# Mixing stage of a two-block transformer kernel: the first pair of attention scores placed after weight unit 14 instead of 13

## The reference, cut to what matters

```python
proj = u @ w_in                     # 1024 -> 5120 columns
q_a, k_a, v_a, q_b, k_b, v_b, g_a, g_b = jnp.split(proj, cuts, axis=-1)
q_a, k_a = partial_rotary(...), partial_rotary(...)
y_a = moba_attention(q_a, k_a, v_a)             # 8 heads, causal softmax here
y_b = stick_breaking_attention(q_b, k_b, v_b)   # 8 heads
merged = gate_a * (y_a @ w_branch_moba) + gate_b * (y_b @ w_branch_sb)
return merged @ w_out
```

## Time and profile before

| | |
|---|---|
| median of three executions | 1198.6 us |
| the profiled execution, its own time | 1198.96 us |
| its span, first to last instruction | 1197.1 us |
| PE busy | 1190.7 us, 99% |
| DVE busy | 782.6 us, 65% |
| ACT busy | 705.6 us, 59% |
| GpSimd busy | 74.1 us, 6% |
| chain that ended last: PE's share | 95% |
| chain that ended last: a DMA transpose of q and k (`qkT`) | 1% |

### The profile page before, as it was taken

How to read it: one execution, slowest core, us unless ns; L and a number is a source line. 1 busy time by engine, 2 the same in 40 slices (tenths; PEclk the granted TensorE clock), 3 DMA queues, 4 the chain that set the end, 5 groups by cost and what they waited for, 6 DMA issues and landing times.

```text
span 1197.1 us, 16770 instructions
## 1 busy us (share of the span) xinstructions
PE 1190.7 (99%) x5582; PEld 983.5 (82%) x5582; DVE 782.6 (65%) x1113; ACT 705.6 (59%) x1035; POOL 74.1 (6%) x119
## 2 busy tenths in 40 slices
PE   9999999999999999999999999999999999999998
PEld 7888888777788888888888788888888888888887
DVE  6655655798676555656778756755656666765554
ACT  7655555776656554557766567655555556655552
POOL 0430000000000000001220110000000000000000
PEclk9999999999999999999999999999999999999999
DMA  9977765795476888755656528977755453876662
GB/s 323 275 225 235 223 197 157 195 186 183 142 224 186 255 252 235 223 171 168 201 172 181 176 70 236 251 225 218 211 168 176 141 181 104 263 225 200 202 198 76
DMA packets 229176, 237.34 MB, mean 198 GB/s; under 512 B 76864, under 2 KB 169152, under 8 KB 229120
## 3 DMA queue, kind: packets, MB, share of 16 engines
q1 hardware_dynamic: 163792, 214.61, 57.2%
q10 hardware_dynamic: 63536, 16.26, 8.2%
q0 software_dynamic: 1792, 5.75, 1.6%
HBM read 219.78 MB, written 1.05 MB: 184 GB/s over the span
## 4 chain that ended last, share of the span: by engine, by line
PE 95%; ACT 1%; DVE 1%; DMA 1%; issue 1%; ACTq 0%; POOL 0%; SPq 0%; POOLq 0%
PE bank L2149 29%; PE bank L2151 29%; PE bank L2150 29%; PE bank L2208 2%; DMA sb_qkT<-sb_qkT 1%; PE bank L2356 1%; PE bank L2611 1%; DVE sb_wl L1444 1%; PE bank L2628 1%; PE bank L2372 1%; PE bank L2343 1%; ACT sb_wh L761 1%; PE bank L2341 0%; ACTq L1041 0%; PE bank L2310 0%
## 5 line engine op out<-in xcount | busy, mean ns | idle before, releaser
L1444 DVE TENSOR_TENSOR sb_wl<-sb_raw,sb_wh 128x1024 fp32r<-128x1024 f32 x313 | 376.4, 1222 | 122.9 <-ACT sb_wh L761 117.7
L2149 PE MATMUL bank<-sb_wh,sb_aTh 128*128 128x512 f32 (+1 forms) x1124 | 435.8, 388 | 0.5 <-DVE sb_aTl L1866 0.4
L2151 PE MATMUL bank<-sb_wh,sb_aTl 128*128 128x512 f32 (+1 forms) x1124 | 430.9, 383 | 0.0
L2150 PE MATMUL bank<-sb_wl,sb_aTh 128*128 128x512 f32 (+1 forms) x1124 | 430.7, 383 | 0.0
L761 ACT ACTIVATE sb_wh<-sb_raw 128x1024 fp32r<-128x1024 f32 (+1 forms) x319 | 327.1, 1047 | 154.1 <-PE bank L2151 101.2
L2149 PEld LDWEIGHTS bank<-sb_wh,sb_aTh 128*128 128x128 f32 x1124 | 211.2, 188 | 42.6 <-DVE sb_aTl L1866 0.8
L2151 PEld LDWEIGHTS bank<-sb_wh,sb_aTl 128*128 128x128 f32 x1124 | 211.2, 188 | 41.8
L2150 PEld LDWEIGHTS bank<-sb_wl,sb_aTh 128*128 128x128 f32 x1124 | 211.4, 188 | 40.2
L1444 DVE TENSOR_TENSOR sb_wl<-sb_z,sb_wh 128x1024 fp32r<-128x1024 f32 x88 | 107.4, 1225 | 55.9 <-ACT sb_wh L761 55.8
L881 ACT ACTIVATE sb_junk<-bank,sb_rstd 128x256 f32<-128x256 f32 x88 | 37.0, 471 | 156.9 <-PE bank L2151 156.7
L1507 DVE SCALAR_TENSOR_TENSOR sb_scores<-bank,sb_rstd,sb_junk 128x256 f32<-128x256 f32 x88 | 38.5, 479 | 118.1 <-ACT sb_junk L881 118.1
(11 more groups left out here) (231 smaller groups left out, 930.3 us busy)
## 6 DMA issues: line engine op xcount, KB each, us to landing
sb_raw<-ffn_w_down SPq DMA_DIRECT2D x80, 256.0 KB, 4.4
sb_raw<-w_in SPq DMA_DIRECT2D x80, 256.0 KB, 3.7
sb_raw<-w_down SPq DMA_DIRECT2D x80, 256.0 KB, 3.9
sb_raw<-w_gate SPq DMA_DIRECT2D x48, 256.0 KB, 3.2
sb_raw<-w_up SPq DMA_DIRECT2D x48, 256.0 KB, 3.9
sb_raw<-ffn_w_gate SPq DMA_DIRECT2D x44, 256.0 KB, 3.6
sb_raw<-ffn_w_up SPq DMA_DIRECT2D x44, 256.0 KB, 4.4
sb_raw<-e_w_in SPq DMA_DIRECT2D x40, 256.0 KB, 3.3
```

Source lines behind the costliest of these rows:

```text
L1444: dve.tensor_tensor(wl[:, u % NSPLIT, :], raws[SLOT[u]], wh[:, u % NSPLIT, :].bitcast(F32), ALU.subtract).then_inc(low_done, 1)
L2149: pe.matmul(dst, lh, w_hi, start=start, stop=False)
L2150: pe.matmul(dst, lh, w_lo, start=False, stop=False)
L2151: return pe.matmul(dst, ll, w_hi, start=False, stop=stop)
```

## The change

One number of the first list is changed. Pair 0 (heads 0 and 1, both stick-breaking) is scored after unit 14 instead of unit 13.

```diff
-        MIX_SCORES = [13, 17, 21, 25, 29, 32, 35, 38]
+        MIX_SCORES = [14, 17, 21, 25, 29, 32, 35, 38]
         MIX_T = [17, 18, 21, 22, 25, 26, 29, 30, 32, 33, 35, 36, 38, 39, 40, 41]
```

## The result

The changed kernel took 1202.66 us at the median of seven runs (1201.1 to 1203.46) against 1198.6 before: ratio 1.0032, 95% interval [1.0022, 1.0042], 4.1 us slower. Predicted were 1200.3 us and a range of 1199.2 to 1201.9, so the direction was right and the size was not. The profiled execution took 1202.5 us with a span of 1200.7.

The account below looks back on a forecast made before the run. TensorE, busy for 99% of the span, was taken to bound the kernel. A removed wait (-0.70 us) and a new one (+2.40) gave +1.7 on 1198.6, so 1200.3 us, range 1199.2 to 1201.9.

Parts of the forecast that it names:

- -0.70 + 2.40: TensorE's removed wait for joined q and k, less 0.70 us, plus a new 2.40 us wait before head 1's transposes.
- The new wait (steps 1 to 7): Chain from pair 0's scores through VectorE and ScalarE to TensorE's transposes of head 1, which wait 2.40 us.
- steps 3 and 4: On VectorE, evac(3), rotate(3) and unit 19's split come before the sums of head 1, which start at 237.88.
- steps 6 and 7: ScalarE's copy pt_step(0), behind unit 21's split and qk_split(2), ends at 243.91; head 1's transposes wait 2.40 us for it.
- What goes: TensorE's wait at pair 0's scores for VectorE's join of turned q and k disappears, gaining at most 0.70 us.
- Rival (b), the clock: TensorE's clock drops in the longer wait before head 1's transposes: 1.96 us more, +3.7 in all, 1202.3 us; chance 0.07.
- Rival (c), a second wait: Slack of 0.6 us before head 3's transposes at step 22 runs out; for one microsecond past it, +2.7, 1201.3; chance 0.10.
- Rival (a), the gain kept: Copy pt_step(0) ends by 241.5, so no new wait before head 1's transposes; 0.7 us gained, 1197.9 us; chance 0.10.

Follow-up runs that it names:

- Experiment 1: Changed kernel, with VectorE's sums of head 1 put back ahead of evac(3) and the rotation at step 16: 1198.62 us, ratio 0.9998.
- experiment 4: Changed kernel, with ScalarE's copy of head 0's turned probabilities moved to the head of step 17: 1200.40 us, ratio 1.0014.
- experiment 6: The kernel before, unchanged, run again over eleven runs: 1198.62 us, ratio 1.0000.
- experiment 10: The changed kernel, unchanged, one further execution: 1202.89 us.
- experiment 7: The changed kernel, unchanged, run again over eleven runs: 1201.58 us, ratio 1.0025.
- experiments 2 to 4: Changed kernel with TensorE's wait filled, 1201.12 us; kernel before with only TensorE's scores moved, 1199.72 us; changed kernel with ScalarE's copy first, 1200.40 us.
- experiment 2: Changed kernel, with eight unused 512-column matmuls on TensorE ahead of the transposes of head 1: 1201.12 us, ratio 1.0018.
- experiments 6, 8 and 9: The kernel before, unchanged, run again (eleven runs, then one execution each): 1198.62, 1198.45 and 1198.95 us.

## Why the prediction was wrong, point by point

Predicted were +1.7 us as -0.70 + 2.40; measured were 4.06. Two steps failed. The removed wait was counted in full and is about nothing near the median, and the fall of the clock, which cost 1.6, stood outside the sum as a rival with a chance of 0.07. The 2.40 was right, and 2.40 + 1.6 is 4.0.

*The new wait (steps 1 to 7).* Right. VectorE takes the scores 0.95 after TensorE starts them (0.96 predicted), the last exp of head 1 starts 11.80 after the scores (11.82), the copy 15.07 (15.16), and the wait by TensorE's starts is 2.68 - 0.23 = 2.45 us (2.40). Experiment 1 took it away by the order of VectorE (steps 3 and 4) and experiment 4 by that of ScalarE (steps 6 and 7).

*What goes.* The removed wait is 0.70 us in the execution that the rows come from, and no typical one. This term was mis-sized: it is 0.0 to 0.1 in three further traces, and near the median about nothing. I subtracted a wait that the landing of a DMA ends as if it were the same in each execution. The time of the profiled run gave no sign of it: it lay 0.36 above the median, but the traced run of experiment 6 lies 0.37 above its own median and has no such wait. Without the term the sum is +2.4 to +2.5: 1201.0 to 1201.1, in the range but at its upper part. Runs of the changed kernel at full clock agree with it (1200.58 to 1201.75, median 1201.12). So this error alone would not have taken the time out of the range.

*Rival (b), the clock.* Together with the missing gain, this took the time out of the range; alone it would have brought the sum to 1201.9, the range's upper end. It was named, but given a chance of 0.07. The kernel before shows a clock of 1.00 across a wait a third as long and a mean of 1.000 over its span of 1197.1 us; that a gap of 2.4 us could bring a fall was my assumption, which nothing in that trace showed. The price put on the fall came near (1.96 predicted; 1.6 in the traces of the result and of experiment 10), in part by luck. The 0.47 a matmul is the length of eight, which holds the last one's tail; by starts it is 0.45 in those rows, and 0.427 in the fall. Those rows are no case of the lower granted clock either, as the trace has 1.00 there (0 to 4 us). And nothing tied the number of slow matmuls behind the wait (seven, and two in part) to those eight. The mean clock is below 1.000 in 6 of the 7 runs of the result, in 4 of 11 in experiment 7, in experiment 10 and in 4 of 5 with a wait of 2.95 us; in none of 33 runs with idle times of 0.48, 0.84 and 1.56 us (experiments 2 to 4). It is given to three digits, which would hide a loss of under some 0.6 us (0.0005 of 1200). Filling the idle time (experiment 2) shows that the idle time, not the lateness, is the cause. In the profile after, the fall followed 2.29 us of idle time, with 0.427 us a matmul, but the four matmuls from 244.75 to 245.45 still started 0.23 to 0.24 us apart, and the lower rate came only behind them.

*Rival (c), a second wait.* Right that it would not come: the only wait in the stage is the one at step 18. Experiment 4 shows how near it was: with TensorE 2.4 us earlier, it came at step 22.

*Rival (a), the gain kept.* Experiment 1 is that case: no wait is left, and nothing measurable is won. Its stage of 148.22 us against 148.19 to 148.31 in experiments 6, 8 and 9 says that little was there to win. None of the versions measurably beats the kernel before.

What stays open: why the same idle time lets the clock fall in one execution and not in the next, why the fall was more frequent in the first seven runs than in experiment 7, and why the transpose lands later in some executions.

## What to carry to other kernels

Where engines walk one list in their own order, a step moved by one place also passes, on each engine, whatever stands there for other reasons: lay out each engine's order at the new place before pricing the wait that goes. Before a wait is counted as a gain, see what ends it: one that a DMA ends can be absent from other executions (here the 0.6 us stood in one profile of four), and more than one profile is needed to know. A new idle gap of TensorE as long as those here (2.3 and 2.95 us; none fell at 1.56) is priced with the clock, as here 1.6 us on top of 2.4, and can cost a different amount in each execution.

## What the runs showed of the hardware

In two traces of the changed kernel (the profile after and experiment 10) the granted clock fell to half after a single idle time of 2.3 us between long busy stretches. It fell 1.4 us after the work had begun again and not in the gap, at about 245.6 and 246.0, and was back at 1.00 by 249.0 and 249.4. In a third trace (experiment 7) the same idle time had no fall behind it. Eight matmuls that nobody needs, put into the idle time, kept the mean clock at 1.000 in eleven runs of eleven. The same 2-byte DMA transpose took from 7.6 to 10.2 us to land in twelve traces of this stage.
